# Convolution taps of the B and C tiles of an SSM layer, on VectorE or on GpSimd

## What is computed

```
def _causal_dwconv(u, w, b):
    y = lax.conv_general_dilated(u, w[:, None, :].astype(u.dtype), window_strides=(1,),
            padding=[(SSM_CONV - 1, 0)], dimension_numbers=('NWC', 'WIO', 'NWC'),
            feature_group_count=u.shape[-1])
    return y + b

zxbcdt = h @ w_in
z, xbc, dt = jnp.split(zxbcdt, [SSM_D_INNER, SSM_D_INNER + SSM_CONV_DIM], axis=-1)
xbc = jax.nn.silu(_causal_dwconv(xbc, conv_w, conv_b))
xs, bm, cm = jnp.split(xbc, [SSM_D_INNER, SSM_D_INNER + SSM_GROUPS * SSM_STATE], axis=-1)
```

## Time and profile before

| what | us |
|---|---|
| median of three executions | 1681.81 |
| the profiled execution, its own time | 1683.25 |
| its span, first to last instruction | 1681.5 |
| TensorE busy, share of the span | 1562.1 (93%) |
| VectorE busy | 1233.8 (73%) |
| ScalarE busy | 1037.6 (62%) |
| GpSimd busy | 56.9 (3%) |

### The profile page before, as it was taken

One profiled execution on the slowest core, in us unless ns is written; L12 is line 12 of the kernel. 1 busy time (PEld: TensorE's weight loads), 2 busy tenths in 40 slices (PEclk: granted clock), 3 DMA queues, 4 the chain that ended last, 5 costly groups with the idle time before them and its releaser, 6 DMA issues.

```text
span 1681.5 us, 21145 instructions
## 1 busy us (share of the span) xinstructions
PE 1562.1 (93%) x7822; PEld 1302.9 (77%) x7822; DVE 1233.8 (73%) x1056; ACT 1037.6 (62%) x894; POOL 56.9 (3%) x93
## 2 busy tenths in 40 slices
PE   5678999998999989899999999999999999999997
PEld 3566888886899977678778778778778788788775
DVE  4454455445488865688888888888788788888897
ACT  4334444334367743677777777777777777777775
POOL 1003300000000000100000000000000000000120
PEclk9878999998999979899999999999999999999999
DMA  7315965553543213899999999999999999999998
GB/s 237 121 51 174 413 251 188 187 189 111 151 126 126 101 66 123 313 359 358 378 362 362 371 372 370 355 369 369 378 351 375 358 363 369 363 365 381 392 351 314
DMA packets 166008, 475.59 MB, mean 283 GB/s; under 512 B 9089, under 2 KB 34961, under 8 KB 165954
## 3 DMA queue, kind: packets, MB, share of 16 engines
q1 hardware_dynamic: 157698, 446.84, 73.1%
q0 software_dynamic: 5680, 18.58, 2.8%
q10 hardware_dynamic: 2576, 9.44, 1.4%
HBM read 453.84 MB, written 20.97 MB: 282 GB/s over the span
## 4 chain that ended last, share of the span: by engine, by line
PE 69%; DVE 15%; issue 7%; ACT 7%; DVEq 1%; DMA 1%; ACTq 1%; SPq 0%
PE bank L649 21%; PE bank L651 21%; PE bank L650 20%; DVE w_lo L1336 7%; ACT w_hi L549 2%; PE bank L964 1%; DVE acc L1267 1%; DVE w_lo L1079 1%; DVE m_hT_lo L1459 1%; ACT m_hT_hi L586 1%; DVE arg L1291 1%; ACT w_hi L408 1%; DMA ring<-swa_w_qkv_in 1%; PE bank L877 1%; DVE xgT_lo L1452 1%
## 5 line engine op out<-in xcount | busy, mean ns | idle before, releaser
L1336 DVE TENSOR_TENSOR w_lo<-ring,w_hi 128x2048 fp32r<-128x2048 f32 x336 | 759.6, 2288 | 110.5 <-ACT w_hi L549 110.4
L549 ACT ACTIVATE w_hi<-ring 128x2048 fp32r<-128x2048 f32 x336 | 642.4, 1919 | 253.3 <-PE bank L651 252.4
L649 PE MATMUL bank<-w_hi,xgT_hi 128*128 128x512 f32 x896 | 355.9, 397 | 28.1 <-DVE w_lo L1336 27.1
L650 PE MATMUL bank<-w_lo,xgT_hi 128*128 128x512 f32 x896 | 349.9, 391 | 0.0
L651 PE MATMUL bank<-w_hi,xgT_lo 128*128 128x512 f32 x896 | 349.8, 390 | 0.0
L1079 DVE TENSOR_TENSOR w_lo<-ring,w_hi 128x2048 fp32r<-128x2048 f32 (+1 forms) x84 | 189.9, 2265 | 174.3 <-ACT w_hi L408 174.0
L408 ACT ACTIVATE w_hi<-ring 128x2048 fp32r<-128x2048 f32 (+1 forms) x84 | 159.2, 1898 | 174.5 <-PE bank L651 172.4
L649 PEld LDWEIGHTS bank<-w_hi,xgT_hi 128*128 128x128 f32 x896 | 168.6, 188 | 75.5 <-DVE w_lo L1336 40.8
L651 PEld LDWEIGHTS bank<-w_hi,xgT_lo 128*128 128x128 f32 x896 | 168.6, 188 | 36.0
L650 PEld LDWEIGHTS bank<-w_lo,xgT_hi 128*128 128x128 f32 x896 | 168.8, 188 | 33.3
L649 PE MATMUL bank<-w_hi,m_hT_hi 128*128 128x512 f32 x448 | 176.9, 395 | 3.0 <-DVE w_lo L1336 3.0
(11 more groups left out here) (291 smaller groups left out, 1706.7 us busy)
## 6 DMA issues: line engine op xcount, KB each, us to landing
ring<-moe_w_gu_in SPq DMA_DIRECT2D x230, 1024.0 KB, 7.2
ring<-moe_w_down_in SPq DMA_DIRECT2D x112, 1024.0 KB, 7.1
ring<-ffn_w_gu_in SPq DMA_DIRECT2D x28, 1024.0 KB, 5.0
ring<-ffn_w_down_in SPq DMA_DIRECT2D x14, 1024.0 KB, 4.8
xg_rows<-zeros POOLq DMA_DIRECT2D x36, 256.0 KB, 12.6
ring<-ssm_w_in_in SPq DMA_DIRECT2D x8, 1024.0 KB, 4.9
ring<-ssm_w_in_in SPq DMA_DIRECT2D x16, 512.0 KB, 3.8
ring<-ssm_w_in_in SPq DMA_DIRECT2D x32, 256.0 KB, 4.2
```

The costliest lines, as they stand in the source:

```text
L549: act.activation(w_hi[:, c % SPLIT], ring[:, c % RING], ACT.Copy).then_inc(hi_ready, 1)
L649: pe.matmul(o, stat[0], mov[0], start=start, stop=False)
L650: pe.matmul(o, stat[0], mov[1], start=False, stop=False)
L1336: dve.tensor_tensor(w_lo[:, c % SPLIT], ring[:, c % RING], w_hi[:, c % SPLIT].bitcast(F32), ALU.subtract).then_inc(lo_ready, 1)
```

## The change

[...] A new semaphore `c_conv_bc` counts the groups done on GpSimd. ScalarE waits for it before the SiLUs and, for the second half of `U`, in place of `c_conv`.

```
+        c_conv_bc = sem("c_conv_bc")
...
             pool_e.wait_ge(rows_cleared, 2 * (3 * E + 3) * 16)
+            term = zeros[:].rearrange("p (i t) -> p i t", i=2)
+            for s in range(G):
+                pool_e.wait_ge(c_u, 2 * s + 2)
+                for tap in range(CONV - 1):
+                    if tap >= 1:
+                        pool_e.drain()
+                    pool_e.tensor_tensor(term, U[:, 2:4, tap:tap + T],
+                                         cwT[:, tap, KI + s:KI + G + s + 1:G].unsqueeze(2).to_broadcast([P, 2, T]),
+                                         ALU.mult)
+                    pool_e.drain()
+                    ins = pool_e.tensor_tensor(acc[:, 2:4], acc[:, 2:4], term, ALU.add)
+                ins.then_inc(c_conv_bc, 1)
             pool_e.wait_ge(rows_ready, TT)
...
                         if s >= 1:
-                            act.wait_ge(c_conv, s)
+                            act.wait_ge(*((c_conv, s), (c_conv_bc, s))[i])
                         act.activation(U[:, 2 * i:2 * i + 2, 3:], bank[i][:].rearrange("p (a b) -> p a b", b=T),
                                        ACT.Copy).then_inc(c_u, 1)
                     ahead(GR0 + 2 * s + (3 if s < G - 1 else 4))
                     act.wait_ge(c_conv, s + 1)
+                    act.wait_ge(c_conv_bc, s + 1)
...
                     for tap in range(CONV - 1):
-                        for i, ct in enumerate((2 * s, 2 * s + 1, KI + s, KI + G + s)):
+                        for i, ct in enumerate((2 * s, 2 * s + 1)):
```

## The result

The changed kernel takes 1695.43 us (median of four, 1694.99 to 1696.01), the kernel before, beside it, 1681.63 us: a ratio of 1.0082, 95% interval 1.0065 to 1.01. The change costs 13.8 us. The forecast was slower by 36.6 us, 1718.4; the direction held, the size did not.

The account below looks back on a forecast made before the run. Bound: a VectorE and ScalarE loop in most grouped steps, TensorE in others. Step 0 5.3, steps 1, 2, 3 and 5 21.2, steps 4 and 6 4.8, step 7 5.3: +36.6 on 1681.81 gives 1718.4 us; range 1683 to 1750.

Parts of the forecast that it names:

- The pace is VectorE's chain to `arg`, then ScalarE.: Grouped steps: VectorE from taps to `arg`, then ScalarE from exponential to `U`, form the 18.73 us loop; delays lengthen it.
- No overlap between GpSimd and VectorE's two-input instructions.: Grouped steps: GpSimd instructions never run beside VectorE's taps, `w_lo` or y·z; alternation had chance 0.60.
- GpSimd's instruction at 1.30 us.: Estimated time of each 512-column GpSimd instruction, from three streams; bounds 0.47 and 2.0 us.
- Six of each alternate, 6 × 1.30 + 6 × 0.43 = 10.4 us.: Start of each step: VectorE taps and GpSimd instructions take turns, so `w_lo` starts at 10.4 instead of 5.08 us.
- δ: Delay of VectorE's chain up to `arg` in a step, forecast as 5.3 us.
- The sum over the steps.: Eight grouped steps: 5.3 + 21.2 + 4.8 + 5.3 = +36.6 us, with steps 4 and 6 at +2.4 each.
- Step 0: TensorE waits for this `w_lo`, +5.3.: First grouped step: TensorE already waits 1.39 us for this weight split, so its delay adds 5.3 us.
- Steps of the later groups near 24 us and equal, TensorE idle in each.: Sign for steps from 3 on: near 24 us each, TensorE idling for `yT_lo` with clock 0.50 behind.
- Nothing behind takes it back.: After the grouped steps: no later work recovers any of the +36.6 us; the DMA ring is full before and after.
- Rival 3, VectorE first: Grouped steps: GpSimd gets in only after taps and `w_lo`, ScalarE waits for it; +44.6 us, 1726; chance 0.14.
- The faster rival: Grouped steps: engines side by side and GpSimd quick, steps 3 to 7 at 17.6 us; −12 us, 1670; chance 0.08.

Follow-up runs that it names:

- splitlate: Kernel before, all taps on VectorE, with the first weight split moved behind `arg` from step 1 on: 1671.17 us, ratio 0.9932.
- nobcpriv: Changed kernel without taps 0 to 2 of B and C or waits for GpSimd, which runs six like instructions on its own tile: 1699.45 us, ratio 1.0103.
- private: Kernel before, twelve taps on VectorE, plus six GpSimd products and additions per step on a tile of its own: 1709.11 us, ratio 1.0161.
- fills: Kernel before, plus six write-only GpSimd fills of 1280 columns per step into an unused tile: 1681.29 us, ratio 0.9999.
- dvefirst: Changed kernel, with GpSimd starting its six instructions only when VectorE's six taps are done: 1727.87 us, ratio 1.0265.
- warm: Changed kernel, plus one GpSimd product and one addition on `zeros`, each with a drain, right behind the clearing of the rows: 1705.93 us, ratio 1.0144.
- aftersplit: Changed kernel, with the first weight split moved behind `arg` from step 1 on: 1706.64 us, ratio 1.0153.
- nobc: Changed kernel without GpSimd's part and the waits for it, leaving out taps 0 to 2 of B and C: 1661.88 us, ratio 0.9882.
- nodrain: Kernel before, plus six GpSimd instructions per step on its own tiles, three result tiles in turn, one drain behind the third: 1710.4 us, ratio 1.0166.

## Why the prediction was wrong

- *The pace is VectorE's chain to `arg`, then ScalarE.* Right for steps 1 to 7. `splitlate` shows it from the other side, and `nobcpriv` that GpSimd's result is not what costs in steps 1 to 6. In step 0 it is.
- *No overlap between GpSimd and VectorE's two-input instructions.* Right (`private`, `fills`, `dvefirst`).
- *GpSimd's instruction at 1.30 us.* Near: 1.04 for the product, 1.27 to 1.29 for the addition, 7.7 us for the six with their drains. The Trainium skill's figure (GPSIMD Engine Reference, "3.1 Elementwise — side-by-side cycle accounting") is for an addition; a quarter of it, 1.12 us, an estimate, is under the 1.27 measured for one.
- *Six of each alternate, 6 × 1.30 + 6 × 0.43 = 10.4 us.* **This term is wrong.** It adds a tap's 0.43 to GpSimd's time for every turn. Measured, a tap delays GpSimd by nothing that the rows show: from a product's start to the addition's there are 1.18 us with taps beside them (513.73 to 514.91) and 1.19 in `dvefirst` (561.89 to 563.08) beside VectorE instructions that read a bank and exclude nothing. The six end after 7.7 us, and the taps with them, at 7.94. A 256-column tap runs on into the start of the next GpSimd instruction, 0.13 us for the first. δ is 2.86 us, not 5.3.
- *The sum over the steps.* Its arithmetic can be checked apart from δ: in `private` δ is 5.4, and steps 1 to 7 grow by 5.8, 5.4, 5.4, 2.5, 5.4, 2.4 and 5.4 us (the last to the end of `yT_lo`), where the forecast had 5.3, 5.3, 5.3, 2.4, 5.3, 2.4 and 5.3. With δ = 2.86 it gives 6 × 2.86 = 17.2 us and nothing in steps 4 and 6. The changed kernel shows 20.7, through step 7: step 0 has 1.3 more (4.2; `warm` has 5.3), step 1 0.5 more behind a slow clock, steps 4 and 6 0.8 and 1.0, which is open.
- *Step 0: TensorE waits for this `w_lo`, +5.3.* 4.2 came, but by luck: there `w_lo` starts at t = 3.49, earlier than before, and what is late is GpSimd's result, which ScalarE waits for. Only `warm`, without the gap, shows the wait as forecast: TensorE waits 4.2 us for the split in place of 1.39, which is δ = 2.8, and the slow clock behind it brings the step to +5.3.
- *Steps of the later groups near 24 us and equal, TensorE idle in each.* Neither: they alternate, 21.6 and 22.4 to 22.6 us, and TensorE idles for `yT_lo` in front of every second set of small matmuls (4.58, 4.57 and 1.88 us), as before.
- *"Nothing behind takes it back."* Wrong, by 6.9 us. From the first transpose of y in step 8 to the scatter of rows there are 81.4 us before (603.93 to 685.32) and 74.5 after (622.59 to 697.05). TensorE's idle time in front is 4.64 us before and 1.88 after; the same small matmuls run at half clock in the one and at full clock in the other, 10.2 us (to 614.13) against 5.8 (to 628.39), and the rest of the gain follows behind them:

```profile
603.93 1.09 PE L825 MATMUL bank<-ident,y 128*128 128x128 f32 x4 [4.64 <-DVE yT_lo L1322]
609.83 3.60 PE L877 MATMUL bank<-tri,dts 128*128 128x128 f32 x16
```

```profile
622.59 0.63 PE L839 MATMUL bank<-ident,y 128*128 128x128 f32 x4 [1.88 <-DVE yT_lo L1336]
625.68 2.00 PE L891 MATMUL bank<-tri,dts 128*128 128x128 f32 x16
```

  In `warm`, whose steps 2 to 6 are nearly those of the changed kernel, the idle time is 3.3 us, the clock 0.50 behind it, and this stretch some 81 us again: most of the 10.5 us between the two. The other runs point the same way, not in strict order: 72.9 to 75.8 us behind 0 to 1.93 us of idle time (`aftersplit`, `private`, `splitlate`), 76.1 to 82.6 behind 2.68 to 6.98 (the other eight). That the clock makes this difference is read from these traces; no run changed the idle time alone. So part of the small loss is luck of where the idle time fell.

The spans add up: 20.7 − 6.9, less 2.1 us by which the profiled execution reached step 0 earlier (455.43 for 457.49; the starts of all traces lie between 454.4 and 457.5, so that is scatter), plus 0.3 behind, is 12.0 = 1693.5 − 1681.5. The profiled execution before lay 1.6 us over its median, which makes up nearly all of the rest to 13.8.

Rival 3, VectorE first, was priced at +44.6 and measured as `dvefirst` at +45.1, by another route than it said: GpSimd ended at t = 12.8, not 14.1, and the late table load made up for it. The faster rival priced at 12 us what `nobc` shows to be worth 19.8, but it needed an engine pair that runs side by side.

## What to carry to other kernels

Before elementwise work goes to GpSimd, look at what VectorE does in the same microseconds: instructions with two inputs in SBUF are stretched to GpSimd's own pace, and six such taps beside six GpSimd instructions cost more (7.9 us) than all twelve on VectorE alone (5.1). Look for the chain that sets the pace and take out what nobody on it waits for; moving one weight split behind `arg` gave 11.6 us without a second engine. Order is then a matter of both ends: the same move lost 11 us where the taps were slow.

## What the runs showed of the hardware

- A GpSimd instruction that reads SBUF and a VectorE instruction with two inputs in SBUF exclude one another until the one that started ends: a tap of 0.43 us takes 1.3 beside products and additions of 512 columns (1.1 to 1.5 each), a product of 1.04 us takes 3.02 behind a split of 2.28. GpSimd fills exclude nothing (5.16 us for twelve taps), nor do VectorE instructions that read the banks.
- A tap of 256 columns in the turn between two GpSimd instructions is free for GpSimd: 1.18 us between starts with it, 1.19 without. y·z, of 512 columns, is not: the product behind it took 1.31 us in place of 1.04 (`dvefirst`).
- Behind the first drain on GpSimd after the clearing of the rows the next instruction came 5.04 to 5.07 us late, once: from 211.8 us in `warm`, from 456.8 in the changed kernel, between fills in `fills`, behind three instructions in `nodrain`. What it waits for is open.
- With a second wait in front of the SiLUs their table load (1.28 us) came behind the wait for GpSimd (521.48, GpSimd's end at 521.42); with one wait it lay ahead of it (525.86, the taps' end at 529.25).
- Behind 1.88 us of idle time TensorE kept its clock of 1.00 (2.4 GHz) through the small matmuls (5.8 us), and so behind 1.93 us in `private` (5.7 us); behind 2.68 us (`nobc`), 2.79, 3.3 and 4.64 us it showed 0.50 in them.
